# Two layers of a hybrid decoder: the halves of the tokens as the inner loop over each weight tile of the split products

## The reference, cut to what matters

```python
def layer_forward(x, c, pos, lw, conv_buf, h0, attn_fn):
    (w_ada_l, b_ada_l, g, w_gu, w_dn, w_in_l, cw, cb, wa, ba, wx, bx, lam, w_o) = lw
    mod = (c @ w_ada_l + b_ada_l).reshape(c.shape[0], N_MOD, -1)
    sh1, sc1, gt1, sh2, sc2, gt2, sh3, sc3, gt3 = [mod[:, m][:, None, :] for m in range(N_MOD)]
    f = swiglu(rms_norm(x, g[0]) * (1 + sc1) + sh1, w_gu[0], w_dn[0])
    x = x + 0.5 * gt1 * rms_norm(f, g[1])
    h = rms_norm(x, g[2]) * (1 + sc2) + sh2
    xl, gl, q, k, v, qi, ki, wi = project(h, w_in_l, pos)
...
    y = jnp.concatenate([y_lru, y_att.astype(h.dtype)], axis=-1) @ w_o
    x = x + gt2 * rms_norm(y, g[3])
    f = swiglu(rms_norm(x, g[4]) * (1 + sc3) + sh3, w_gu[1], w_dn[1])
    x = x + 0.5 * gt3 * rms_norm(f, g[5])
    return x, (k, v, ki, hT, new_buf)
```

## Time and profile before

| | |
|---|---|
| three runs | 3287.28, 3287.92 (median), 3289.07 us |
| span of the profiled execution | 3289.0 us |
| TensorE matmuls, busy | 87% of the span, 20506 instructions |
| TensorE weight loads | 80%, 20506 |
| VectorE | 45% |
| ScalarE | 24% |
| GpSimd | 5% |
| mean granted TensorE clock | 0.886 |

### The profile page before, as it was taken

How to read it: one execution, slowest core, us unless ns; L and a number is a source line. 1 busy time by engine, 2 the same in 40 slices (tenths; PEclk the granted TensorE clock), 3 DMA queues, 4 the chain that set the end, 5 groups by cost and what they waited for, 6 DMA issues and landing times.

```text
span 3289.0 us, 56073 instructions
## 1 busy us (share of the span) xinstructions
PE 2866.4 (87%) x20506; PEld 2643.8 (80%) x20506; DVE 1465.7 (45%) x2006; ACT 782.9 (24%) x1076; POOL 158.8 (5%) x299
## 2 busy tenths in 40 slices
PE   5999997987778669999979999969796768699997
PEld 4999896976545669999969998969575548699997
DVE  2333124365799443332243331244648983533312
ACT  2233023220012133332223321222200122333221
POOL 0000001001320000000000000010113100000000
PEclk8999998975579789999989999989656888899998
DMA  6223632212353012322243226222123421123231
GB/s 183 82 85 89 176 88 79 73 43 61 112 148 109 26 39 83 89 85 74 87 123 89 84 82 186 85 72 75 48 69 110 146 86 40 42 85 89 69 88 62
DMA packets 524666, 291.09 MB, mean 89 GB/s; under 512 B 20673, under 2 KB 518882, under 8 KB 524162
## 3 DMA queue, kind: packets, MB, share of 16 engines
q1 hardware_dynamic: 513154, 266.35, 27.9%
q0 software_dynamic: 11392, 23.23, 2.4%
HBM read 285.75 MB, written 3.77 MB: 88 GB/s over the span
## 4 chain that ended last, share of the span: by engine, by line
PE 78%; DVE 7%; issue 6%; SPq 3%; DMA 2%; ACT 2%; DVEq 0%; POOL 0%; ACTq 0%; POOLq 0%
PE ps L581 19%; PE ps L583 19%; PE ps L582 19%; PE ps L703 4%; PE ps L592 4%; PE ps L553 3%; PE ps L701 3%; DMA sb_wslot<-w_ada 2%; PE ps L819 2%; SPq L433 2%; SPq L431 1%; PE ps L563 1%; ACT sb_h L864 1%; PE ps L723 1%; DVE sb_h L1149 1%
## 5 line engine op out<-in xcount | busy, mean ns | idle before, releaser
L582 PE MATMUL ps<-sb_h_lo,sb_w_hi 128*128 128x272 f32 x3360 | 974.4, 290 | 0.0
L581 PE MATMUL ps<-sb_h_hi,sb_w_hi 128*128 128x272 f32 x2816 | 818.7, 291 | 54.3 <-DVE sb_h_lo L1135 54.3
L583 PE MATMUL ps<-sb_h_hi,sb_w_lo_ffn 128*128 128x272 f32 x2816 | 820.8, 291 | 0.0
L874 ACT ACTIVATE sb_w_hi<-sb_wslot 128x1024 fp32r<-128x1024 f32 (+2 forms) x322 | 332.9, 1036 | 1485.9 <-PE ps L583 1337.0
L1110 DVE TENSOR_TENSOR sb_w_lo_ffn<-sb_wslot,sb_w_hi 128x1024 fp32r<-128x1024 f32 (+1 forms) x272 | 324.0, 1194 | 794.6 <-ACT sb_w_hi L874 794.0
L582 PEld LDWEIGHTS ps<-sb_h_lo,sb_w_hi 128*128 128x128 f32 x3360 | 642.3, 191 | 0.5
L581 PEld LDWEIGHTS ps<-sb_h_hi,sb_w_hi 128*128 128x128 f32 x2816 | 535.1, 190 | 59.4 <-issue 54.2
L583 PEld LDWEIGHTS ps<-sb_h_hi,sb_w_lo_ffn 128*128 128x128 f32 x2816 | 534.5, 190 | 0.0
L581 PE MATMUL ps<-sb_act_hi,sb_w_hi 128*128 128x272 f32 x1408 | 408.7, 290 | 11.1 <-DVE sb_w_lo_ffn L1110 11.1
L583 PE MATMUL ps<-sb_act_hi,sb_w_lo_ffn 128*128 128x272 f32 x1408 | 407.6, 290 | 0.0
L582 PE MATMUL ps<-sb_act_lo,sb_w_hi 128*128 128x272 f32 x1408 | 407.3, 289 | 0.0
(11 more groups left out here) (218 smaller groups left out, 3199.7 us busy)
## 6 DMA issues: line engine op xcount, KB each, us to landing
sb_wslot<-ffn_w_gu SPq DMA_DIRECT2D x176, 512.0 KB, 3.7
sb_wslot<-w_ada SPq DMA_DIRECT2D x144, 512.0 KB, 4.7
sb_wslot<-ffn_w_down SPq DMA_DIRECT2D x64, 512.0 KB, 3.9
sb_wslot<-w_in SPq DMA_DIRECT2D x32, 512.0 KB, 3.7
sb_wslot<-ffn_w_down SPq DMA_DIRECT2D x32, 384.0 KB, 3.4
sb_down<-key_pages POOLq DMA_DIRECT2D x128, 96.0 KB, 2.2
sb_down<-key_pages SPq DMA_DIRECT2D x128, 96.0 KB, 2.0
sb_wslot<-w_out SPq DMA_DIRECT2D x16, 512.0 KB, 3.9
```

The costliest lines, as they stand in the source:

```text
L581: mm(out, wh, xh, start=(kc == 0), stop=False)
L582: mm(out, wh, xl, start=False, stop=False)
L583: last = mm(out, wl, xh, start=False, stop=(kc == of - 1))
L874: act_fn(w_hi[s][:, 0:rows, 0:cols], wslot[i][:, 0:rows, 0:cols], ACT.Copy).then_inc(w_hi_done.sem, 1)
```

## The change

In `piece`, the loop over the two halves b moves from the outside (around kc) to the inside (around each matmul). Before, all 24 matmuls of half 0 run, then all 24 of half 1, and for each kc the order is hi x w_hi, lo x w_hi, hi x w_lo. After, for each kc the six matmuls are hi x w_hi for half 0 and half 1, lo x w_hi for both, hi x w_lo for both. The wait for h_parts stands before each second kc, as before, and is now followed by both halves. The start and stop flags follow the same matmuls.

```diff
-                for b in range(2):
-                    for kc in range(k0, k1):
-                        wh, wl = w_hi[s][:, kc - k0, :], w_lo[s][:, kc - k0, :]
-                        if norm is not None and b == 0 and kc % 2 == 0:
-
-                            pe.wait_ge(h_parts.sem, h_parts.at(l_[0], norm * DC + kc + 2))
-                        xh, xl = (v[:, kc, b * TH:(b + 1) * TH] for v in (hi, lo))
-                        out = ps[:, 2 * pair + b, 0:TH]
-                        mm(out, wh, xh, start=(kc == 0), stop=False)
-                        mm(out, wh, xl, start=False, stop=False)
-                        last = mm(out, wl, xh, start=False, stop=(kc == of - 1))
+                for kc in range(k0, k1):
+                    if norm is not None and kc % 2 == 0:
+
+                        pe.wait_ge(h_parts.sem, h_parts.at(l_[0], norm * DC + kc + 2))
+                    wh, wl = w_hi[s][:, kc - k0, :], w_lo[s][:, kc - k0, :]
+                    for w, v in ((wh, hi), (wh, lo), (wl, hi)):
+                        for b in range(2):
+                            last = mm(ps[:, 2 * pair + b, 0:TH], w, v[:, kc, b * TH:(b + 1) * TH],
+                                      start=(kc == 0 and v is hi and w is wh), stop=(kc == of - 1 and w is wl))
                 last.then_inc(w_used[s].sem, 1)
```

## The result

The changed kernel takes 3269.6 us (median of 4 runs, 3265.1 to 3272.8) against 3288.1 (4 runs, 3287.3 to 3289.1): a ratio of 0.9950, 95% interval 0.9937 to 0.9963, 18.5 us less. The forecast was 12.8 us less, 3275.1, in a range of 3262 to 3290. The profiled execution is the fastest of the four: its span is 3263.5 us. A run's time is 1.5 to 2.2 us longer than its span in every run that lists both, so the profiled execution of the kernel before, with its span of 3289.0 us, took about 3290.6 us (an estimate): not at the upper end of the runs but above all four. So of the 25.5 us between the two spans some 7 come from which executions were profiled (2.5 before, 4.5 after); 18.5 is the measure of the change. Two runs beside the experiments took far longer than all others (the kernel before, 6159.8 us, and e2, 5483.6 us); they are left out.

The account below looks back on a forecast made before the run. TensorE, busy 87% of the span, was taken as the bound. First pieces behind norms save 12.8 us, pace and other costs 0: 3287.9 us becomes 3275.1, range 3262 to 3290.

Parts of the forecast that it names:

- What stays: Split products: same matmuls, operands and weight loads, no added DMA, semaphore or instruction, nothing new waited for; cost nothing.
- The first piece behind each norm: Six pieces waiting for h: each wait releases 12 matmuls, at most 12 follow the last, not 30; saves 12.8 us.
- r: Time from a first piece's first matmul until the clock rises to full; taken as 5.3 us, giving pieces of 8.47 us.
- The pace inside a piece: All 15072 split matmuls: alternating banks and keeping the weight tile change the pace by 0; bound 7.5 us either side.
- The sign given for a right forecast: Gate-up product: 1591 matmuls, give or take 6, in 200 us if the forecast holds.
- the bank hazard: Rival: a stall on rewriting one's own bank vanishes, pace 0.1132 us, 188 us more saved, 3087 us; chance 0.08.
- The clock does not drop between alternating banks: Denies the rival that alternating banks lowers the clock, 0.10 us more per slow matmul, up to 3427 us; chance 0.03.
- The pace did not get worse: Denies the rival that the new order averages 0.1272 us a matmul, adding 22.6 us, 3297.7 us; chance 0.09.
- Little is left: Rival: clock rises where it did, only 4.8 us saved, or a longer pace takes most; say 3285 us; chance 0.16.
- The lower end that the rival gives: Fastest time in the range of the rival that little is left, 3280.6 to 3290.6 us.
- the late rise: Six first pieces: the clock rises where it did before, so only 4.8 us are saved.
- Does it reach the end?: Behind the first pieces: TensorE sets the pace and loads move up; a lost cover gives back at most 2.3 us per stage.

Follow-up runs that it names:

- e2: Against the kernel before: new order everywhere except in the code with the wait for h, which keeps the old order; 3280.5 us, 0.9983.
- e1: Against the kernel before: new order only in the code with the wait for h (first piece of each loop round), old order elsewhere; 3272.2 us, 0.9961.
- e3: Against the kernel before: in all pieces kc outside, the half inside it, the three matmuls of a half together; 3281.9 us, 0.9984.
- e6: The changed kernel plus 22 useless matmuls ahead of each first piece behind a norm; 3261.5 us, 0.9929 of the kernel before.
- e8: The kernel before, old order, plus 22 useless matmuls ahead of each first piece behind a norm; 3287.0 us, 1.0009.
- e7: The changed kernel with a wait for each chunk of h plus 22 useless matmuls ahead of each first piece; 3256.4 us, 0.9916 of the kernel before.
- e10: The kernel of e3 run and traced once more, against the kernel before; 3280.7 us, 0.9980.

## Why the prediction was right, point by point

- *What stays*: right. The counts of matmuls and loads are the same (20506 each), and ScalarE's next copy starts when the first piece ends, at 83.34 instead of 86.80; nothing of the gain in these pieces was lost behind them.
- *The first piece behind each norm*: right, in mechanism and size. The sum was 12.8 us, the trace has 12.8 and e1 alone 12.2. r was taken as 5.3; the six rises came 5.0 to 5.5 us behind the first matmul. The second group of twelve found its chunks there in each piece. That the tenth agrees is luck: r was picked between 3.2 and 9.2 by one stage of six, and in the five traces with this order and this wait the six pieces gain 12.1 to 14.2 us, with single rises as early as 2.8.
- *The pace inside a piece*: the term that was mis-sized. I took 0, with 7.5 us as the bound; 7.1 us less were measured in the trace, and e2 shows nearly the same by itself (7.6 in the trace, 5.8 in the runs). The sign given for a right forecast, 1591 matmuls give or take 6 in 200 us, was missed by 2: there are 1599. The crossing in rows 7 had been read to a hundredth of a microsecond, and the effect is 0.6 ns a matmul: 200/1591 - 200/1599. Rows of that resolution could not have shown it; the difference between two products in rows 4 was the right measure for the bound, and 0 the wrong value in it.
- *The rivals*: the bank hazard is not it: the pace did not go to 0.1132 us, but by a twentieth of the way. The clock does not drop between alternating banks: it is 1.00 in the 200 us above, with the bank changing at every matmul and TensorE busy throughout. The Trainium skill's case of it (TensorE: Matmul & The Clock Gate, "A second HAM failure mode: psum-queue depth-cycling"), in which TensorE idled in tiny gaps between groups, does not occur in the trace of this loop. The pace did not get worse, except in e3's gate-up products.
- *Little is left*: no. The clock rose earlier behind the first matmul than in five of the six stages before, and the pace got shorter, not longer. (The lower end that the rival gives, 3280.6, follows from none of its terms: the late rise alone gives 3287.9 - 4.8 = 3283.1.)
- *Does it reach the end?*: yes. The rest of the products didn't get longer, and what lies between them changed by 1.8 us.
- The change gained 5.5 us more than forecast, and the pace, taken as 0, is the term that was missing: 12.8 + 7.1 = 19.9 us by the traces' two terms, 18.5 by the medians. The 1.4 us between these are less than executions of one kernel differ by.

## What to carry to other kernels

When a product starts on operands that are still being made, let each arriving piece of them release all the matmuls that can use it: run the loop over what is ready inside, and wait for the smallest unit (the wait for each chunk was worth another 11 us). Count what is left behind the last arrival, at the granted clock of that stretch, and look at where that clock rises and falls in each piece, not in one: it differs between pieces of the same code. Extra matmuls ahead of the piece helped with the new order (e6), not with the old one (e8), and not where the wait was per chunk already (e7). Reusing a stationary tile was no gain by itself in this kernel, where every matmul loads its tile anyway.

## What the runs showed of the hardware that was not expected

- Work ahead of a piece did not by itself hold the clock: with 22 matmuls ahead, groups of six matmuls with gaps between them lost it 1.8 to 1.9 us behind the first one in the three pieces that began with it (1223.70 to 1225.59, busy for 1.00 of 1.89 us), while the new order kept it in the four pieces that began with it (e6, busy for 6.74 of 7.10 us).
- At full clock, a 272-column matmul with its own load takes 0.1257 us in one order and 0.1251 in another (1591 and 1599 in 200 us), and the better order isn't the same for every product (e3: 1589 in 200 us of a gate-up product, where the changed kernel has 1599, but 563 in 70 us of a down product, where it has 562). e10, the same kernel as e3, has 1588 and 563.
- Executions of the same kernel differ by more than the first three runs suggested: the kernel before took 3278.8 to 3294.4 us in the runs beside the experiments, the changed one 3265.1 to 3272.8.
